# First phase of a fused transformer-layer kernel: split fp32r projections, modulation rows on VectorE, later q and k transposes

## What is computed

```python
mod_x = (jax.nn.silu(c) @ w_mod[l] + b_mod[l])[:, None, :]
sh1, sc1, g1, sh2, sc2, g2 = jnp.split(mod_x, N_MOD, axis=-1)
hx = modulate(x, norm_mix_g[l], sh1, sc1)
hc = modulate(ctx, norm_mix_g[l], csh1, csc1)
fx, qx, kx, vx = split_projection(hx @ w_in[l])
fc, qc, kc, vc = split_projection(hc @ w_in[l])
qx = axial_rope(heads(qx, N_Q_HEADS, q_norm_g[l]), row, col)
...
x = x + g1 * (jnp.concatenate([four_x, attn_x], axis=-1) @ w_out[l])
x = x + g2 * expert_choice_ffn(modulate(x, norm_ffn_g[l], sh2, sc2), ...)
return rms_norm(x, final_norm_g)
```

## Time and profile before

| | us |
|---|---|
| median of 3 runs | 2188.39 (2185.91 to 2189.53) |
| the profiled execution, device time | 2189.9 |
| its span in the trace | 2188.1 |
| PE busy / DVE busy / ACT busy in the span | 1969.8 / 1576.8 / 1259.7 |
| first latent projection starts | 83.6 |
| rows begin on PE / end of first phase | 292.2 / 361.9 |
| attention starts on PE / expert phase begins / first expert matmul | 397.1 / 1003.9 / 1060.3 |

### The profile page before, as it was taken

How to read it: one execution, slowest core, us unless ns; L and a number is a source line. 1 busy time by engine, 2 the same in 40 slices (tenths; PEclk the granted TensorE clock), 3 DMA queues, 4 the chain that set the end, 5 groups by cost and what they waited for, 6 DMA issues and landing times.

```text
span 2188.1 us, 28420 instructions
## 1 busy us (share of the span) xinstructions
PE 1969.8 (90%) x8917; PEld 1486.1 (68%) x8917; DVE 1576.8 (72%) x1985; ACT 1259.7 (58%) x1830; POOL 271.7 (12%) x305
## 2 busy tenths in 40 slices
PE   6899988898899889981699999999999999999993
PEld 2444467566666666651588888888888888888882
DVE  0255541577666766656798999889998899888993
ACT  1222110567665766552477777777767777777762
POOL 0122210011110111010120110101101011010111
PEclk9899999899999999995799999999999999999996
DMA  8411155501110111002799999999999999999985
GB/s 259 155 77 77 58 192 187 129 27 49 58 41 26 48 58 41 26 19 106 269 410 393 384 379 382 390 390 386 381 376 396 384 393 377 379 385 394 379 322 199
DMA packets 107298, 513.31 MB, mean 235 GB/s; under 512 B 12488, under 2 KB 37488, under 8 KB 56944
## 3 DMA queue, kind: packets, MB, share of 16 engines
q1 hardware_dynamic: 99728, 489.34, 58.3%
q0 software_dynamic: 4608, 16.78, 3.0%
q10 hardware_dynamic: 2912, 6.55, 0.8%
HBM read 479.09 MB, written 33.55 MB: 234 GB/s over the span
## 4 chain that ended last, share of the span: by engine, by line
PE 48%; issue 2%; DVE 2%; DMA 1%; POOL 0%; ACT 0%; ACTq 0%; POOLq 0%; SPq 0%
PE banks L1402 31%; PE banks L1427 15%; PE banks L1414 1%; PE banks L1383 1%; DVE topi L1275 1%; DVE top L1273 1%; DVE cand L1276 0%; DMA xe<-h_scratch,idx_g 0%; DMA acc_scratch<-ysc,idx_s 0%; DVE raw L1366 0%; DMA fgain<-in_final_norm_g 0%; ACT raw L1259 0%; DMA raw<-acc_scratch 0%; POOL carry L1153 0%; POOL idx_g L1158 0%
## 5 line engine op out<-in xcount | busy, mean ns | idle before, releaser
L1307 DVE TENSOR_TENSOR w_lo<-raw,w_hi 128x2048 fp32r<-128x2048 f32 x256 | 574.8, 2287 | 67.7 <-ACT w_hi L1208 67.7
L1208 ACT ACTIVATE w_hi<-raw 128x2048 fp32r<-128x2048 f32 x256 | 470.2, 1917 | 7.6 <-DMA raw<-in_w_exp 7.5
L1402 PE MATMUL banks<-w_hi,x_hi 128*128 128x512 f32 x1024 | 405.5, 396 | 1.4 <-DVE x_lo L1301 1.4
L1402 PE MATMUL banks<-w_hi,x_lo 128*128 128x512 f32 x1024 | 400.1, 391 | 0.0
L1402 PE MATMUL banks<-w_lo,x_hi 128*128 128x512 f32 x1024 | 399.5, 390 | 0.0
L1315 DVE TENSOR_TENSOR d_lo<-raw,d_hi 128x1024 fp32r<-128x1024 f32 x256 | 296.2, 1218 | 2.1 <-ACT d_hi L1230 2.0
L1230 ACT ACTIVATE d_hi<-raw 128x1024 fp32r<-128x1024 f32 x256 | 258.0, 1060 | 35.0 <-DMA raw<-in_w_exp 20.0
L1402 PEld LDWEIGHTS banks<-w_hi,x_lo 128*128 128x128 f32 x1024 | 192.8, 188 | 40.8
L1402 PEld LDWEIGHTS banks<-w_hi,x_hi 128*128 128x128 f32 x1024 | 193.0, 188 | 39.7 <-DVE x_lo L1301 1.8
L1402 PEld LDWEIGHTS banks<-w_lo,x_hi 128*128 128x128 f32 x1024 | 193.2, 189 | 38.2
L908 DVE TENSOR_TENSOR ptl<-banks,pth 128x384 fp32r<-128x384 f32 x320 | 176.3, 554 | 56.8 <-ACT pth L854 51.8
(11 more groups left out here) (195 smaller groups left out, 2627.3 us busy)
## 6 DMA issues: line engine op xcount, KB each, us to landing
raw<-in_w_exp SPq DMA_DIRECT2D x384, 1024.0 KB, 7.7
unit<-in_w_mod SPq DMA_DIRECT2D x12, 1024.0 KB, 7.8
q_scratch<-qst SPq DMA_DIRECT2D x8, 1536.0 KB, 5.2
win<-in_w_mod SPq DMA_DIRECT2D x12, 1024.0 KB, 12.4
qt<-q_scratch SPq DMA_DIRECT2D x32, 384.0 KB, 4.2
win<-in_w_in SPq DMA_DIRECT2D x2, 2048.0 KB, 13.5
xt<-in_x SPq DMA_DIRECT2D x8, 512.0 KB, 3.3
xr<-in_x SPq DMA_DIRECT2D x8, 512.0 KB, 4.0
```

The lines of the kernel that those rows point to most:

```text
L1208: act.activation(w_hi[which][c][:, :], raw[which][c][:, :], ACT.Copy).then_inc(s["hi_done"], 1)
L1307: dve.tensor_tensor(w_lo[which][c][:, :], raw[which][c][:, :], w_hi[which][c][:, :].bitcast(F32), ALU.subtract).then_inc(s["lo_done"], 1)
L1402: i = pe.matmul(psum[:, 2 * (j % 2) + which, :], x_[par][:, k, :], w_, start=(k == 0 and w_ is hi and x_ is x_hi), stop=(k == KD - 1 and x ...
```

## The change

- **Projection**: the weights `w_in` and the modulated tile are split into a rounded part (ScalarE copy to fp32r) and a remainder (VectorE subtraction), and each plain matmul becomes three fp32r ones: high by high, high by low, low by high.
- **Rows**: VectorE multiplies each unit by a per-partition scalar and accumulates over 8 steps in `acc` (two buffers, even and odd units); PE sums over partitions with one matmul by ones; ScalarE copies the result to the first partition of `acc`; GpSimd adds that partition to `mod_scratch` in DRAM by DMA. Two units are done in each step of a latent tile. `rows` are read back at the start of attention and finished on GpSimd.
- **Order**: the loop is written out by tile. q and k are no longer split before their transposes but after (ScalarE copy, VectorE subtraction), 8 transposes in place of 28, put between the second and the third projection chunk of the next tile.
- q and k leave by DMAs on SP from half the partitions each; attention reads q with two DMAs in place of one. `w_mod` and `w_in` are laid out in DRAM by unit. The first eight units have a buffer each.
- **Expert phase**: `fgain` is scaled at the end, and the first gather is issued from the index table without the copy and the carrier.

```diff
...
           "q_norm_g", "k_norm_g", "w_out", "w_router", "final_norm_g"]
...
+def column_units(w, n):
...
-    q_d = dram("q_scratch", [TL, P, NQ * 2 * P], F32)
+    q_d = dram("q_scratch", [TL, NQ, HD, 2 * P], F32)
+    mod_d = dram("mod_scratch", [4 * D], F32)
     h2_d = dram("h2_scratch", [N, D], F32)
...
+                sp.dma_start(vec[r:r + v.shape[0], :], v).then_inc(s["small_in"], 16)
...
+                sp.dma_start(slot[u][:, :, :].rearrange("p k n -> p (k n)"), w_mod[u]).then_inc(unit_in[u], 16)
+            for c in (2, 1, 0):
+                sp.dma_start(w_raw[:, c, :, :].rearrange("p k n -> p (k n)"), w_in[c]).then_inc(w_raw_in[c], 16)
...
+            def load(i):
+                if i < RING:
+                    sp.wait_ge(s["unit_used"], NC_UNITS)
+                else:
+                    sp.wait_ge(s["mod_used"], i - RING + 1)
+                half = w_mod[NC_UNITS + i // 2][:, i % 2 * HALF_UNIT:(i % 2 + 1) * HALF_UNIT]
+                sp.dma_start(ring[i % RING][:, :], half).then_inc(ring_in[i % RING], 16)
...
+            def store(n):
+                sp.wait_ge(s["qlo_done"], qt_count(n + 1))
...
+            for n in range(TS + 2):
+                units = units_of(n) if n < TS else ()
+                for i in range(2 * units[0], 2 * units[0] + 3) if units else ():
+                    load(i)
+                if n >= 2:
+                    store(n - 2)
+                if units:
+                    load(2 * units[0] + 3)
...
+            def row_out(u):
+                if u == 0:
+                    pool.wait_ge(s["preset"], 16)
+                pool.wait_ge(s["row_ev"], u + 1)
+                pool.dma_start(mod_d[u * UM:(u + 1) * UM].unsqueeze(0), acc[u % 2][0:1, :], accum_op=ALU.add).then_inc(row_out_done[u % 2], 16)
...
+            for n in range(TS + 1):
+                if n + 1 < TS:
+                    rstd(n + 1)
+                if n >= 1:
+                    squares(n - 1)
+                    rstd16(n - 1)
+                    for u in units_of(n - 1)[1:]:
+                        row_out(u)
+                if n < TS:
+                    for u in units_of(n)[:1]:
+                        row_out(u)
...
+            def weights(c, half):
+                act.wait_ge(w_raw_in[c], 16)
+                if c < 2:
+                    act.wait_ge(s["unit_used"], 2 if c == 1 else 4)
+                k = slice(4 * half, 4 * half + 4)
+                act.activation(w_hi[:, c, k, :], w_raw[:, c, k, :], ACT.Copy).then_inc(s["wh_done"], 1)
...
+            def queries(n):
+                after(act, s["k_out"], 64 * n)
+                after(act, s["q_out"], 32 * (n - TC))
+                for b in range(0 if lat(n) else 1, 2):
+                    c0 = 0 if lat(n) or b == 0 else 2 * P
+                    act.wait_ge(s["qt_done"], qt_count(n) + (b + 1 if lat(n) else 1))
+                    act.activation(qst[:, 4 * b + c0 // P:4 * b + 4, 0, :],
+                                   psum[:, QT + b, c0:].rearrange("p (h n) -> p h n", n=P), ACT.Copy).then_inc(s["qhi_done"], 1)
...
+            def row(u):
+                act.wait_ge(s["row_mm"], u + 1)
+                act.activation(acc[u % 2][0:1, :], psum[0:1, MB, 0:UM], ACT.Copy).then_inc(s["row_ev"], 1)
...
+            for n in range(TS + 2):
+                if 1 <= n <= TS:
+                    out2(n - 1)
+                if n + 1 < TS:
+                    normal(n + 1)
+                if n >= 2:
+                    queries(n - 2)
+                if n < TC:
+                    for half in range(2):
+                        weights(1 - n, half)
+                if n < TS and lat(n):
...
+                if 1 <= n <= TS:
+                    for u in units_of(n - 1)[1:]:
+                        row(u)
+                if n + 1 < TS:
+                    turn(n + 1, 0)
+                if n < TS and lat(n):
+                    out0(n)
+                if n + 1 < TS:
+                    turn(n + 1, 1)
+                    if n + 2 < TS:
+                        load_x(n + 2)
+                    high(n + 1)
+                if n < TS:
+                    for u in units_of(n)[:1]:
+                        row(u)
+                if n + 2 < TS:
+                    square(n + 2)
...
+            def modulation(u, half):
+                i = 2 * u + half
+                dve.wait_ge(ring_in[i % RING], 16 * (i // RING + 1))
+                if half == 0:
+                    after(dve, row_out_done[u % 2], 16 * (u // 2))
+                else:
+                    dve.wait_ge(s["mod_used"], i)
+                for k in range(4):
+                    w = ring[i % RING][:, k * UM:(k + 1) * UM]
+                    c = c_sig[:, 4 * half + k, 0:1]
+                    if half == 0 and k == 0:
+                        ins = dve.tensor_scalar(acc[u % 2][:, :], w, c, None, ALU.mult)
+                    else:
+                        ins = dve.scalar_tensor_tensor(out=acc[u % 2][:, :], in0=w, scalar=c, in1=acc[u % 2][:, :], op0=ALU.mult, op1=ALU.add)
+                    if k < 3:
+                        link(ins)
+                ins.then_inc(s["mod_used"], 1)
...
+            for n in range(TS + 2):
+                if 1 <= n <= TS:
+                    values(n - 1)
+                if n >= 2:
+                    queries(n - 2)
+                if 1 <= n <= TS:
+                    scaled(n - 1)
+                units = units_of(n) if n < TS else ()
+                for u in units[:1]:
+                    modulation(u, 0)
+                    modulation(u, 1)
+                if 1 <= n <= TS:
+                    sums(n - 1)
+                for u in units[1:]:
+                    modulation(u, 0)
+                if 1 <= n <= TS:
+                    rotate(n - 1)
+                for u in units[1:]:
+                    modulation(u, 1)
+                if n < TC:
+                    for half in range(2):
+                        weights(1 - n, half)
+                if n + 1 < TS:
+                    low(n + 1)
...
+                for k in range(KD):
+                    for x_, w_ in ((h_hi, w_hi), (h_hi, w_lo), (h_lo, w_hi)):
+                        i = pe.matmul(psum[:, PJ + c, :], x_[n % 2][:, k, :], w_[:, c, k, :], start=(k == 0 and x_ is h_hi and w_ is w_hi),
+                                      stop=(k == KD - 1 and x_ is h_lo))
+                i.then_inc(s[f"pj{c}"], 1)
...
+            def row(u):
+                pe.wait_ge(s["mod_used"], 2 * u + 2)
...
+                pe.matmul(psum[0:1, MB, 0:UM], ones[:, 0:1], acc[u % 2][:, :], start=True, stop=True).then_inc(s["row_mm"], 1)
...
+            for n in range(TS):
+                if not lat(n):
+                    project(n, 2)
+                    turn(n + 1, 0)
+                    turn(n + 1, 1)
+                else:
+                    project(n, 1)
+                    for u in units_of(n - 1)[1:]:
+                        row(u)
+                    if n + 1 < TS:
+                        turn(n + 1, 0)
+                    project(n, 0)
+                    if n + 1 < TS:
+                        turn(n + 1, 1)
+                    row(units_of(n)[0])
+                    queries(n - 1)
+                    project(n, 2)
+                if n == 1:
+                    queries(n - 1)
+            row(NR_UNITS - 1)
+            queries(TS - 1)
...
+            sp.dma_start(rows[:, :, :].rearrange("p a d -> p (a d)"), mod_d.partition_broadcast(P)).then_inc(s["rows_in"], 16)
+            sp.dma_start(x2[:, :], a["norm_ffn_g"][0].partition_broadcast(P)).then_inc(s["rows_in"], 16)
...
+            pool.wait_ge(s["rows_in"], 32)
+            pool.tensor_scalar(rows[:, SC2, :], rows[:, SC2, :], 1.0, ROOT, ALU.add, ALU.mult).then_inc(s["scale_done"], 1)
+            pool.wait_ge(s["scale_done"], 1)
+            pool.tensor_tensor(rows[:, SC2, :], rows[:, SC2, :], x2[:, :], ALU.mult).then_inc(s["rows_done"], 1)
...
-                after(pool, s["x_in"], 16 * e)
+                if isinstance(e, int) and e == 0:
+                    pool.indirect_dma_start(out=xe[:, :], out_offset=None, in_=h2_d,
+                                            in_offset=bass.IndirectOffsetOnAxis(ap=icol[:, 0:1], axis=0)).then_inc(s["x_in"], 16)
+                    return
+                pool.wait_ge(s["x_in"], 16 * e)
                 pool.tensor_copy(idx_g[:, :], icol[:, bass.ds(e, 1)]).then_inc(s["idx_g"], 1)
-                pool.wait_ge(s["idx_g"], e + 1)
+                pool.wait_ge(s["idx_g"], e)
                 after(pool, s["x_mm"], 2 * e)
-                carrier(e if isinstance(e, int) and e < 3 else 2 * e - 2)
...
-            dve.wait_ge(s["fg_in"], 16)
-            dve.tensor_scalar(fgain[:, :], fgain[:, :], ROOT, None, ALU.mult)
...
+            dve.wait_ge(s["fg_in"], 16)
+            dve.tensor_scalar(fgain[:, :], fgain[:, :], ROOT, None, ALU.mult)
```

More of the change, by code:

```diff
@@ L1093, in nc_phase_m @@
     NX = TL
[L1094 to L1095 removed]
+    xa_in = unit_in
```

(1 more changed line is left out.)

715 lines of the change are left out of this document (315 added, 400 removed).

## The result

The changed kernel takes 2160.44 us (median of 4 runs, 2157.44 to 2164.65) against 2188.37 us for the kernel before. The ratio is 0.9875, its 95% interval 0.9857 to 0.9894: 28 us or 1.25% faster. The forecast was 2176.5 us, 12 us faster. The measured time lies within the stated range of 2138 to 2200 us, but the gain is more than twice the one forecast.

What follows compares the result with a forecast made beforehand. TensorE was taken to pace the old latent tiles, a ring of waits the new loop. First phase -4.8 and other edits -7.1 took the profiled 2189.9 to 2178 us; the median, 1.5 lower, gave 2176.5, range 2138 to 2200.

Steps and rivals of the forecast that it cites:

- The ring: Latent loop: a cycle of waits between engines, from one tile's chunk 2 end to the next's, sets a 33.2 us step.
- X: Latent loop: time from issue of the odd unit's write-out to its landing, taken as 3.6 us, ends 2.1 and 6.2.
- the write-out binds: Its denial was a rival: write-out lands within the power's wait, step 27.7 us, total 2138 us; chance 0.10.
- TensorE is not the bound: Its denial was a rival: TensorE sets the latent step at 19.3 us, total 2079 us; chance 0.04.
- nothing slower came of it: Refers to the slower rival: write-out as slow as the scatter, 6.2 us, step 35.8 us, total 2195 us; chance 0.16.
- the rival without a loss from the clock: Latent loop: TensorE loses nothing to a cold clock, 18 us less, total 2158 us; chance 0.05.
- start of the latent projections: First phase before the loop: the first latent projection starts at about 81 us (80.5 in the sum), against 83.6 before.
- first latent step: Start of the loop, nothing to write out: TensorE's 19.3 us and 2.5 for a cold start, 21.8 us.
- the rest of seven steps: Second to eighth latent tile without the write-out's landing time: 29.6 us a step, less 1.1 us in the first.
- behind the last projection: After the loop: 18 us to the last subtraction, then six SP issues of 2.5 and a landing of 3, 23.5 us.
- step = 29.6 + X us: Latent loop: all waits of one step summed, 33.2 us with X at 3.6, 7 more than a tile before.
- the 2.6 us for the clock: Latent loop: TensorE's loss, once a step, to the lower clock on transposes and what follows its idle time, 2.6 us.

Runs made afterwards that it cites:

- write-out early: Changed kernel with the odd unit's write-out issued ahead of GpSimd's power instead of behind it: 2127.92 us.
- three buffers: Changed kernel with three buffers for the row sums in place of two, nothing moved: 2126.13 us.
- transposes late: Changed kernel with the q and k transposes of the tile before moved behind the third projection chunk: 2110.79 us.
- both moves: Changed kernel with the write-out issued ahead of the power and the q and k transposes behind the third chunk: 2087.24 us.
- fillers: Changed kernel with 72 extra discarded matmuls in each of seven steps where TensorE waits for the rotation: 2146.55 us.
- plain matmuls: Changed kernel with projections as 8 plain float32 matmuls a chunk on the rounded values, remainders computed but unused: 2171.99 us.
- no units: Changed kernel with the sixteen rows units (loads, VectorE work, sums over partitions, write-outs) left out of the loop: 2083.06 us.
- x tile late: Changed kernel with the next x tile's load issued some 3 us later on ScalarE, behind rounding and the even row's copy: 2158.41 us.
- the expert edits alone: Kernel before with only the two expert-phase edits (final gain scaled at the end, first gather issued from the index table): 2182.62 us.

## Why the prediction was right and wrong

**Right: what the loop is.** The ring, its order, the write-out behind the power, TensorE's idle time of some 11 us (it was 10.2) and the cold clock behind it stood in the prediction. The runs agree with it: with the step of 31.9 us and X of 3.3 us from the changed kernel's trace, the ring gave write-out early, three buffers, transposes late, both moves and fillers to within 2 to 8 us, plain matmuls and no units to within 6 and 14. The rivals fell: the write-out binds, TensorE is not the bound, and nothing slower came of it. The measured 2160 us lies by chance next to the 2158 of the rival without a loss from the clock, but the clock costs 14 us. Two signs were off: the loop's granted clock is 0.82 and not about 0.9, and TensorE is busy 68% of it and not near 60%, in part because matmuls at the lower clock take longer.

**Wrong: the sum.** The first phase was to end at 357.1 and ended at 345.67, 11.4 us earlier. By its terms:

| term | forecast | measured | difference |
|---|---|---|---|
| start of the latent projections | 80.5 | 77.8 | -2.7 |
| first latent step | 21.8 | 20.1 | -1.7 |
| X, seven times | 25.2 | 22.9 | -2.3 |
| the rest of seven steps | 206.1 | 200.3 | -5.8 |
| behind the last projection | 23.5 | 24.6 | +1.1 |

The step that failed is thus "step = 29.6 + X us" with its 33.2 us: it was 31.9 on average, 8.1 us of the 11.4 over seven steps. Within it no term is far off. X was 3.3, not 3.6; the stretch from chunk 2's end to the power's end was 13.1, not 13.5 (the copies and the gain scaling ahead of the even unit were done 0.4 us sooner); the last step has no next tile to normalise and lacks 0.9 more. Transposes and chunk 2 took 8.9 against 9.05: the 2.6 us for the clock was right there. The prices that it took without a row for the even unit, 0.36 us for the first operation and 0.5 for the others, were right (0.35 and 0.485). All but one of the terms erred on the long side, and the one behind the loop hides two errors that cancel: from the last projection to SP's first issue of q it was 16.7 us and not 18, but the six issues took 5.6 us and not 2.5. The forecast gain of 4.8 us in this phase was the difference of two sums of over 350 us, and an error of 4% in a step that occurs seven times was larger than it.

**X by its bounds.** The fixed part taken from the earlier trace rows, 2.1 us, was right to a tenth, as the runs with the x tile late and the plain matmuls show. The 2.15 to 2.22 us with the x tile late agree with what the Trainium skill (DMA: Bandwidth & Descriptors, on the anatomy of a GpSimd DMA) states, about 2.0 us. What I added to it from the gather and the scatter is no property of the write-out, but what other transfers issued around it do, mostly the x tile's load; the forecast never asked what else is issued in those 3 us. That 3.6 came near to the measured 3.3 is luck.

**The other edits.** The earlier selection gave 3.4 of the 3.5 forecast. The gather gave 2.5 in place of 4.0: its issue took 2.9 us beside VectorE's splits, the case named as the lower bound (2). Attention's +0.4 was +0.75 (4.13 from q's issue to the first matmul, 3.37 before). The sum missed that TensorE starts the Fourier part 3.5 us behind VectorE's first operation there, where it was 5.5 before; in both kernels it waits there for the Fourier matrices. Their loads are now issued 0.4 us sooner after the phase's start and take 5.4 us at the median in place of 6.2; why they are faster stays open.

**What lies outside.** Attention was 2.0 us shorter. Its tiles take 72.3 us or 73.4 to 73.9 in both kernels, and the longer ones have a granted clock of 0.98 and not 1.00:

```profile
542.50:614.75 72.25, 65.05 (x338) 46.81 (x338) 50.68 (x122) 47.27 (x128) 10.77 (x12) 1.00 0.14 44
614.75:688.23 73.48, 66.72 (x339) 48.32 (x338) 50.94 (x122) 47.31 (x128) 10.76 (x12) 0.98 0.14 43
```

Which tiles they are, and how many, differs between the profiled kernels, and with it the time from attention's first matmul to its last store's issue: 586.8 to 590.4 us over the twelve kernels with the new attention, 589.3 in the changed one. So most of these 2.0 us are put down to that, not to the change. The two kernels with the old attention have 591.3 (before) and 590.8 us (the expert edits alone), just above all twelve, so some tenths of a microsecond a tile may belong to the change; no run separates them. The medians hold another 2.7: the profiled execution lay 4.2 us above the median after, and 1.5 before.

In sum, of the 16 us by which the forecast missed, 11.4 are in the first phase, 1.5 between it and attention, 2.0 in attention and 2.7 in the medians, and the gather takes 1.6 back.

## What to carry to other kernels

Follow the ring and not the busy times: here TensorE gave up 4.4 us of work a tile and the step won 1.1 of them, while the place of one write-out was worth 32 us and the place of eight transposes 50 (4 of these through the write-out that it sped up). When work is moved into the gaps of a loop, look for what it waits for there; a buffer that is freed by a DMA issued a moment before puts the DMA's whole latency on the path, here 2.1 to 5.1 us. And where a forecast is the small difference of two long sums, its error is that of the sums.

## What the hardware showed beyond this

- **Idle time has a second price.** After 10 us idle, the next 9 us of TensorE ran at a mean granted clock of 0.79 and cost 2 us more; 72 matmuls without use bought 14 us. Short gaps cost it too, but not all. With the units left out, the stretch behind the gap stayed at full clock after 1.6 us idle and in three of the six cases of 2.5 us; in the other three it took 9.0 us in place of 7.4. With the fillers it was short after up to 2.6 us, and after 2.9 us it took 10.2.
- **A small DMA waits for what was issued just ahead of it.** Without 29 loads of 512 KB, a 1 KB write-out with an x tile 0.6 us ahead took 2.8 to 3.1 us, against 3.1 to 3.4 and once 5.1 with them. With that one 512 KB load moved to 1 us behind it, it took 2.2 in six of seven steps. Behind 384 KB of q issued 0.25 us ahead it took 3.8.
- **An issue can take a wait over.** Beside VectorE's splits, GpSimd's copy took 2.15 us and the gather's issue after it 1.22; with the copy gone, the issue itself took 2.9.
